# Moving the turned 32-column blocks of three feed-forward nets from SBUF to SBUF, in place of a round trip through DRAM

## What is computed

```
def swiglu(x, w_gu, w_down):          # x: 256 x 1024, w_gu: 1024 x 5632, w_down: 2816 x 1024
    g, u = jnp.split(x @ w_gu, 2, axis=-1)
    return (jax.nn.silu(g) * u) @ w_down

x = x + 0.5 * swiglu(rmsnorm(x, ffn1_norm), ffn1_w_gu, ffn1_w_down)   # f1
...                                                                   # three mixers, gates, w_out
x = x + 0.5 * swiglu(rmsnorm(x, ffn2_norm), ffn2_w_gu, ffn2_w_down)   # f2
...                                                                   # a short convolution with gates
x = x + g2 * swiglu_2(modulate(rmsnorm_2(x, norm2_g), sh2, sc2), ffn_w_in, ffn_w_out)   # f3
```

## Time and profile before

| | |
|---|---|
| median of the runs | 889.99 us (889.35 to 891.33) |
| profiled execution: from its first to its last instruction (the page gives no other time for it) | 888.8 us |
| TensorE busy, matmuls | 877.8 us, 99% |
| VectorE, ScalarE, GpSimd busy | 631.1, 460.4, 43.4 us |
| moved by DMA | 215.04 MB, 94158 packets |
| read from and written to HBM | 204.58 and 9.72 MB |
| DMAs spill / reload | 72 / 18 |

### The profile page before, as it was taken

One profiled execution on the slowest core, in us unless ns is written; L12 is line 12 of the kernel. 1 busy time (PEld: TensorE's weight loads), 2 busy tenths in 40 slices (PEclk: granted clock), 3 DMA queues, 4 the chain that ended last, 5 costly groups with the idle time before them and its releaser, 6 DMA issues.

```text
span 888.8 us, 11079 instructions
## 1 busy us (share of the span) xinstructions
PE 877.8 (99%) x4079; PEld 732.2 (82%) x4079; DVE 631.1 (71%) x883; ACT 460.4 (52%) x697; POOL 43.4 (5%) x66
## 2 busy tenths in 40 slices
PE   9999999999999999999999999999999999999996
PEld 7888887888998888888888888888888888888885
DVE  6788879837558877688578887765768766665743
ACT  6644556625688475446545545454445344444530
POOL 0000010022103000000000000001000100000000
PEclk9999999999999999999999999999999999999999
DMA  9999999874654454454699999965655577777741
GB/s 362 336 331 341 373 339 345 298 249 134 182 176 173 164 192 166 147 186 143 218 313 344 342 333 331 333 247 169 251 180 178 180 245 241 241 234 248 247 120 47
DMA packets 94158, 215.04 MB, mean 242 GB/s; under 512 B 13800, under 2 KB 45464, under 8 KB 93976
## 3 DMA queue, kind: packets, MB, share of 16 engines
q1 hardware_dynamic: 93384, 212.90, 69.9%
q10 hardware_dynamic: 720, 1.44, 0.4%
HBM read 204.58 MB, written 9.72 MB: 241 GB/s over the span
## 4 chain that ended last, share of the span: by engine, by line
PE 94%; DMA 2%; DVE 2%; issue 1%; ACT 1%; POOL 0%; SPq 0%; POOLq 0%; DVEq 0%
PE ps L739 29%; PE ps L740 29%; PE ps L741 29%; PE ps L677 1%; PE ps L654 1%; DMA t_raw<-in_f_up 1%; PE ps L647 1%; DMA t_tp<-inner_rows 1%; PE ps L856 1%; PE ps L872 1%; PE ps L814 0%; PE ps L848 0%; DMA t_acc<-in_xT 0%; PE ps L796 0%; DVE t_wl L1207 0%
## 5 line engine op out<-in xcount | busy, mean ns | idle before, releaser
L1207 DVE TENSOR_TENSOR t_wl<-t_raw,t_wh 128x1024 fp32r<-128x1024 f32 (+3 forms) x308 | 359.9, 1203 | 106.8 <-ACT t_wh L914 105.9
L914 ACT ACTIVATE t_wh<-t_raw 128x1024 fp32r<-128x1024 f32 (+3 forms) x308 | 307.6, 1040 | 110.3 <-DMA t_raw<-in_f_up 71.8
L739 PE MATMUL ps<-t_wh,t_XH 128*128 128x512 f32 (+2 forms) x640 | 249.8, 390 | 0.0
L741 PE MATMUL ps<-t_wh,t_XL 128*128 128x512 f32 (+2 forms) x640 | 247.0, 386 | 0.0
L740 PE MATMUL ps<-t_wl,t_XH 128*128 128x512 f32 (+2 forms) x640 | 246.7, 385 | 0.0
L741 PEld LDWEIGHTS ps<-t_wh,t_XL 128*128 128x128 f32 x640 | 120.1, 188 | 24.0
L740 PEld LDWEIGHTS ps<-t_wl,t_XH 128*128 128x128 f32 x640 | 120.3, 188 | 22.8
L739 PEld LDWEIGHTS ps<-t_wh,t_XH 128*128 128x128 f32 x640 | 120.2, 188 | 22.8
L739 PE MATMUL ps<-t_wh,t_YH 128*128 128x512 f32 x288 | 113.1, 393 | 0.2 <-DVE t_YL L1632 0.2
L741 PE MATMUL ps<-t_wh,t_YL 128*128 128x512 f32 x288 | 112.2, 389 | 0.0
L740 PE MATMUL ps<-t_wl,t_YH 128*128 128x512 f32 x288 | 112.1, 389 | 0.0
(11 more groups left out here) (225 smaller groups left out, 615.8 us busy)
## 6 DMA issues: line engine op xcount, KB each, us to landing
t_raw<-in_f_up SPq DMA_DIRECT2D x130, 512.0 KB, 5.1
t_raw<-in_f_dn SPq DMA_DIRECT2D x66, 512.0 KB, 5.1
t_raw<-in_ada SPq DMA_DIRECT2D x48, 512.0 KB, 5.6
inner_rows<-t_tp SPq DMA_DIRECT2D x60, 128.0 KB, 3.9
t_tp<-inner_rows SPq DMA_DIRECT2D x15, 512.0 KB, 4.0
t_raw<-in_mkv SPq DMA_DIRECT2D x8, 512.0 KB, 4.5
t_raw<-in_ga SPq DMA_DIRECT2D x8, 512.0 KB, 3.2
t_raw<-in_gc SPq DMA_DIRECT2D x8, 512.0 KB, 3.2
```

Source lines behind the costliest of these rows:

```text
L739: pe.matmul(o, xh, h, start=k == 0, stop=False)
L741: x = pe.matmul(o, xl, h, start=False, stop=k == n - 1)
L914: act.activation(wh[:, m % SPL, lo:w], raw[:, n % RAW, lo:w], ACT.Copy).then_inc(hi_made, 1)
L1207: dve.tensor_tensor(wl[:, n % RAW, lo:w], raw[:, n % RAW, lo:w], wh[:, m % SPL, lo:w].bitcast(F32), ALU.subtract).then_inc(drained, 1)
```

## The change

Each pair's four spills and one reload are replaced by one step `swap`: sixteen DMAs from one SBUF buffer, `tp`, into another. The other is `gathered`: the unused buffer `grow` in f1, the first half of `hn` in f2 and f3. DMA (i, j) takes the 32 partitions of quarter i and those of their columns that belong to quarter j, 2 runs of 128 values (512 bytes; 256 bytes in pair 5) in each partition, 32 KB. They are issued in four rounds d, with j = (i + d) mod 4. `swap` stands where `spill` stood, but one unit later for q = 5. `inner` stands at unit 8q + 12 for q = 4 too. New waits: SP's swap of pair q waits until DVE has read the gathered rows of pair q - 1 (`hid_lo`), and DVE's `blocks` of pair q until the DMAs of pair q - 1 have all landed (`swapped`), because they read `tp`.

```diff
-            ways = (3, 4, 6) if (f, q) == ("f1", 0) else (0, 1, 3 if q == 4 else 4)
-            out.extend((step, f, q) for step, late in zip(("spill", "reload", "inner"), ways) if u == first + late)
+            ways = (3, 6) if (f, q) == ("f1", 0) else (q == 5, 4)
+            out.extend((step, f, q) for step, late in zip(("swap", "inner"), ways) if u == first + late)
...
-        spilled, reloaded = sem("spilled"), sem("reloaded")
+        swapped = {f: sem(f"swapped_{f}") for f in FFNS}
...
+        def gathered(f, n):
+
+            return (grow if f == "f1" else hn[:, 0, :])[:, 0:n]
+
-        def placed(q, t):
+        def placed(f, q, t):
 
             n = inner_width(q)
-            return tp[:, 0:n].rearrange("p (i t c n) -> p t c i n", i=4, t=2, n=32)[:, t]
+            return gathered(f, n).rearrange("p (i t c n) -> p t c i n", i=4, t=2, n=32)[:, t]
...
             def inner(f, q):
-                act.wait_ge(reloaded, 16 * (inner_no(f, q) + 1))
+                act.wait_ge(swapped[f], 256 * (q + 1))
...
                 dve.wait_ge(*hid_made.at(f, 2 * q + (q < 5), 1))
+                if q:
+                    dve.wait_ge(swapped[f], 256 * q)
                 dve.transpose(tp[:, 0:2 * n].rearrange("p (t n) -> p t n", t=2), hp[:, :, 0:n]).then_inc(*blocked.by(f, q))
...
-            def spill(f, q):
+            def swap(f, q):
 
                 n = inner_width(q)
                 sp.wait_ge(*blocked.at(f, q))
-                for i in range(4):
-                    rows = inner_rows[i, :, :, 0:n // 8].rearrange("b f e -> f b e")
-                    sp.dma_start(rows, tp[32 * i:32 * i + 32, 0:n].rearrange("f (b e) -> f b e", b=8)).then_inc(spilled, 16)
-
-            def reload(f, q):
-
-                n = inner_width(q)
-                sp.wait_ge(spilled, 64 * (inner_no(f, q) + 1))
-                rows = inner_rows[:, :, :, 0:n // 8].rearrange("i (t j) f e -> (j f) (i t) e", t=2)
-                sp.dma_start(tp[:, 0:n].rearrange("p (b e) -> p b e", b=8), rows).then_inc(reloaded, 16)
+                if q:
+                    sp.wait_ge(*hid_lo.at(f, q - 1, 1))
+                for d in range(4):
+                    for i in range(4):
+                        j = (i + d) % 4
+                        rows = tp[32 * i:32 * i + 32, 0:n].rearrange("f (t j e) -> f t j e", t=2, j=4)[:, :, j]
+                        sp.dma_start(gathered(f, n)[32 * j:32 * j + 32, :].rearrange("f (i t e) -> f i t e", i=4, t=2)[:, i],
+                                     rows).then_inc(swapped[f], 16)
```

More of the change, by code:

```diff
@@ L482, in build @@
         drop = nc.dram_tensor("mod_rows", (48, P), F32, kind="Internal").ap()
-        inner_rows = nc.dram_tensor("inner_rows", (4, 8, 32, P), F32, kind="Internal").ap()
         def sem(name):
@@ L993, in inner @@
             def inner(f, q):
-                act.wait_ge(reloaded, 16 * (inner_no(f, q) + 1))
+                act.wait_ge(swapped[f], 256 * (q + 1))
                 for t in (0, 1):
-                    act.activation(parts_of(HH, q, t), placed(q, t), ACT.Copy).then_inc(*hid_hi.by(f, q, t))
+                    act.activation(parts_of(HH, q, t), placed(f, q, t), ACT.Copy).then_inc(*hid_hi.by(f, q, t))
             def squares(p, j, t):
@@ L1339, in inner @@
                     dve.wait_ge(*hid_hi.at(f, q, t))
-                    dve.tensor_tensor(parts_of(HL, q, t), placed(q, t), parts_of(HH, q, t).bitcast(F32),
+                    dve.tensor_tensor(parts_of(HL, q, t), placed(f, q, t), parts_of(HH, q, t).bitcast(F32),
                                       ALU.subtract).then_inc(*hid_lo.by(f, q, t))
@@ L1865, in _ @@
                     "load_cond": load_cond, "ada_rows": ada_rows, "load_mod": load_mod,
-                    "load_mid": load_mid, "gate": gate, "load_final": load_final, "final": final, "spill": spill, "reload": reload}
+                    "load_mid": load_mid, "gate": gate, "load_final": load_final, "final": final, "swap": swap}
             for name, *args in SCHEDULE:
```

## The result

The forecast was +1.1 us; the change costs 62. The kernel after takes **951.56 us** in the median of 4 runs (950.09 to 952.86), the kernel before 889.67 beside it (4 runs, 889.04 to 891.33): a ratio of **1.0699** with the interval 1.0686 to 1.0711. The profiled execution of after took 950.09 us and spans 948.4; before's spans 888.8 us (the table of the time before). So the two traces differ by 59.6 us, and I account for that.

What follows compares the result with a forecast made beforehand. TensorE's matmuls, 99% of the span, were taken as the bound, with 1.5 us to gain. Terms 0.1 (f1's pair 1), 0.3 (pair 2) and 0.7 (pairs 4 and 5) gave +1.1: 890.0 to 891.1 us, range 888.4 to 897.5.

Steps and rivals of the forecast that it cites:

- the first rival: f1 and f2: sixteen issues on SP hold the fetches behind; 11 us at 0.60 per issue, put at 896; chance 0.42.
- The pace of an issue: SP's swap: 0.48 us per issue, 7.7 us for sixteen; lower end 0.34, upper end 0.60, 9.6 us.
- The 7.7 us of pair 1: f1's pair 1: swap from 55.4 to 63.1, unit ready at 68.6, used at 68.60; stop of 0 to 0.1 us.
- my working at 0.60: f1's pair 1: a stop of 1.9 us if each issue takes 0.60 us.
- pair 3 "loses nothing": f1's pair 3: a backlog of transfers covers its issues, so no loss; what follows comes 2.4 us sooner.
- f2's pair 5 has "0.3 to spare": f2's pair 5: unit 52 ready at 568.2, used at 568.46, nothing lost; 3.5 us late at 0.60 per issue.
- the other pairs of f2: f2 outside pairs 4 and 5: DMA load between f1's and f3's; nothing taken for them.
- the +0.7 of pairs 4 and 5: f1's pairs 4 and 5 together: between +2.2 and -0.2 us, taken as +0.7.
- The wait of `blocks`: Wait for the sixteen: costs nothing in f1's pair 5 unless rows land over 2 us later; nothing in other pairs.
- the landing: Swap's end: 2 us from the last issue to the landing, between 1.8 and 7.3.
- the rows' latency: Swap to `inner`: rows land 9.7 us after the swap's start, 10.1 now; no gain and no loss.
- the last rival: Every full pair: the sixteen DMAs serialize, 29 us per pair in place of 10.1, time 1040; chance 0.02.

Runs made afterwards that it cites:

- The pads: Kernel before plus eight unused 2 KB DMAs from SBUF behind each pair's four spills: 924.39 us to SBUF, 908.14 us to DRAM.
- pair 1 alone: Changed kernel with eight DMAs per pair, half of the inner blocks left out, but sixteen in f1's pair 1: 895.34 us, ratio 1.0067.
- places of before: Changed kernel with inner of pair 4 and the swap of pair 5 each one unit earlier: 943.23 us, ratio 1.0606.
- eight issues: Changed kernel with rounds d = 0 and 1 alone, half of the inner blocks left out: 890.04 us, ratio 1.0005.
- four and twelve: Changed kernel with four DMAs of each swap issued by SP and twelve by GpSimd, whole output: 899.50 us, ratio 1.0113.
- with eight: Changed kernel with eight DMAs of each swap issued by SP and eight by GpSimd, whole output: 892.68 us, ratio 1.0034.

## Why the prediction was wrong

The place and the mechanism stood in the text, as the first rival: SP's queue becomes the bound, behind the sixteen issues in f1 and f2. It was given 0.42, and 11 us where 62 were measured. Its 11 was the sum at a pace of 0.60, so the pace by itself, the first step below, makes up about ten of the 61 us by which the forecast was short. The rest lies in the steps after it. What failed, step by step:

1. **The pace of an issue.** "I take 0.48, the pace of f1's own rows." The rows were spills, with DRAM as their destination; measured are 0.60, and 0.64 with the step between two, above the 0.60 of the upper end. The swap is 10.2 us and not 7.7. The pads, once to SBUF and once to DRAM, show that the destination makes the difference. The price came from rows that were alike in shape but not in what they join.
2. **Each pair was worked out from before's rows.** The 7.7 us of pair 1 were laid behind 55.4, its start in the kernel before. But the swap of pair 0, which the prediction did not treat at all, made pair 1 start at 60.20, 4.8 later, while TensorE wanted the unit only 1.2 later (76.71 - 6.88 = 69.83 against 68.60). Lateness was handed on: 1.9 us by my working at 0.60, 1.59 measured with pair 1 alone in the way (with TensorE 1.4 late, as said there), 6.88 with all. For pairs 4 and 5 I did carry lateness from one to the next; the same had to be done from pair 0 on. That pair 3 "loses nothing" (3.88 us measured), that f2's pair 5 has "0.3 to spare" and that the other pairs of f2 cost nothing fell by the same step: five of the ten stops lie in f2.
3. **A stop was priced as its own length.** No term stood for the clock. Every stop of 3.4 us or more had 3.4 to 6.8 us at the 1.2 GHz level beside it, about 17 us in all, over a quarter of the loss. Before's row showed only a stop of 1.46 with no drop, so nothing in the sum warned of it.
4. **The places and new waits.** They were named, and all that they do was put into the +0.7 of pairs 4 and 5. SP's waits have a new row for `HL`, and `blocks` waits for the swap, once in each net, in pair 5 (us, times; the first with the longest):

```profile
SPq L1821 <- DVE t_HL L1345: 12.3, 3, 5.3
```

```profile
  ACT t_HH L999: 32.5, 7
  DVE t_tp L1340: 12.3, 3
```

   The wait of `blocks` was priced rightly at nothing. In the other pairs it never held. In f1's pair 5 it held DVE for 4.0 us, but the blocks were turned by 155.4, and the weight tile of unit 48 came to ACT only at 159.5:

```profile
154.70 0.71 DVE L1340 STREAM_TRANSPOSE t_tp<-t_hp 128x512 f32<-128x512 f32 x1 [4.00 <-DMA t_grow<-t_tp]
...
159.51 1.06 ACT L917 ACTIVATE t_wh<-t_raw 128x1024 fp32r<-128x1024 f32 x1 [11.49 <-DMA t_raw<-in_f_dn]
```

   The cost is SP's: pair 5's swap waits for `HL` of pair 4 (in f1 it begins at 163.10), and each fetch behind with it. Putting the places back let that swap begin 5.5 us sooner in f2 (603.87 for 609.41) and gave 8.3 us in all. The steps of `inner` and of the swap were moved together, so the share of each stays open.
5. **The range.** It ended at 897.5 because I took 0.55 for the pace and added lateness up in proportion. The loss is not in proportion: eight issues cost nothing, sixteen cost 62 us.

What held: the landing ("2 us", measured 1.8/1.9/4.6 after an issue); the rows' latency (ACT waits for them 32.5 us in 7 in the row above, 34.8 in 14 before); f3 without a stop; HBM writes of 1.07 MB; the reload gone from SP's waits. The serializing of the last rival did not come: in f1's pair 1 the sixteen were issued 0.64 us apart and from the fourth on landed so, each 1.9 after its issue, three in flight at a time; with a sixteenth of the bytes a landing took 1.8 in the median in place of 1.9 and the kernel as long. The Trainium skill's rule named there ("SBUF — State Buffer", section "Can I just issue two DMAs to hit both halves?") gives a gain of 6% from a second transfer, and DMAs whose bytes count for 0.1 us do not test it.

**Open.** Why an issue with SBUF at both ends is longer; whether one of 128 partitions costs the same 0.60, which would let fewer DMAs carry the swap (not tried: the turned blocks change partitions in groups of 32); what GpSimd's queue stands still for.

## What to carry to other kernels

The queue that issues the fetches is a resource like any engine: count what stands between one fetch and the next, in us, against the spare time of the fetch behind, and ask whether the pair before leaves that spare time intact. Within that time issues cost nothing (eight per pair here). Beyond it a us can return several times (f1's pair 1 alone: a stop of 1.6 us, 5.3 us of the kernel's time), as a late fetch, as a late start of the next group, and as matmuls at 1.2 GHz. Here four spills, a reload and a wait of 2.6 us between them were cheaper for SP than sixteen issues without a wait.

## What the runs showed of the hardware that was not expected

- SP's issue takes 0.60 us in the median from SBUF to SBUF, whether 2 or 32 KB, one run or two (0.51 at least, with one run); the 2 KB from the same source to DRAM take 0.42. All of these have 32 partitions at the source.
- GpSimd's pauses come by the count of its issues. With sixteen per pair they stand in f1 after the 25th, the 50th and the 75th (pair 1 after 9, pair 3 after 2, pair 4 after 11), and again so in f2 and f3; with twelve per pair after the 25th and 50th, with eight after the 25th. They last 2 to 7 us. Some shorter ones, 0.2 to 0.4 us in most, fall elsewhere. GpSimd's timeline in f1's pair 2 with twelve per pair (24 lie ahead of these rows):

```profile
75.67 0.54 POOL L1763 DMA_DIRECT2D t_grow<-t_tp  x1 [15.73 <-DVE t_tp L1343]
80.46 5.80 POOL L1763 DMA_DIRECT2D t_grow<-t_tp  x11 [4.26 <-issue]
```

- The clock did not follow the length of a stop alone: 1.79 us (156.47, four and twelve) had 3.4 us at half clock behind it, 2.78 us (140.76, the same kernel) and 2.90 us (104.76, places of before) none. The window behind the stop of 1.79, in that kernel:

```profile
156.60:160.00 3.40, 3.40 (x9) 2.64 (x10) 3.40 (x6) 3.40 (x6) 0.00 (x0) 0.50 1.04 422
```
